# Products of constants on TensorE in the tails of the norms of a six-mixer network

## The chip, the cores and the metric

The kernel runs as one launch on one core of a Trainium2 chip. The metric is the device time of an execution in microseconds, lower is better. A core has a matrix engine (TensorE, here PE), a vector engine (VectorE, here DVE), a scalar engine (ScalarE, here ACT), a third elementwise engine (GpSimd, here POOL) and a queue for transfers (SyncE, here SP). Each engine works through its own instructions in the order in which they are written and stops only at waits for semaphores, which other engines count up.

## The reference

The reference passes 256 tokens of width 1024 through two layers of one block (a hybrid of a gated delta rule and attention, then a conformer convolution, each followed by a SwiGLU network) and four layers of a second (HGRN2, mLSTM, S5, HGRN2, each followed by a SwiGLU network). What matters here are the norms between these stages:

```python
def rms_norm(x, gain):
    xf = x.astype(F32)
    y = xf * lax.rsqrt(jnp.mean(jnp.square(xf), axis=-1, keepdims=True) + EPS)
    return (y * gain.astype(F32)).astype(x.dtype)
...
        h = h + gt1 * rms_norm(y, g_mix_post[layer])
        f = swiglu_ffn(modulate(rms_norm(h, g_ffn_pre[layer]), sh2, sc2), w_ffn_in[layer], w_ffn_out[layer])
        h = h + gt2 * rms_norm(f, g_ffn_post[layer])
...
def _layernorm(x, g, b):
    xf = x.astype(jnp.float32)
    mu = jnp.mean(xf, axis=-1, keepdims=True)
    xc = xf - mu
    var = jnp.mean(xc * xc, axis=-1, keepdims=True)
    return (xc * lax.rsqrt(var + LN_EPS) * g + b).astype(x.dtype)
```

In the first block a branch's output is normed and added to the residual, and the residual is normed again ahead of the next branch. In the second block the sum of residual and branch goes through one layer norm, and the result is the residual and the next input at once.

## The kernel before

Activations lie feature-major: eight chunks of 128 features on the partitions, 256 tokens along the free axis. A projection is a sum of products of a 128x128 weight tile with a 128x256 chunk. The weights come from memory in 341 slabs of 1 MB through a ring. Most projections split their operands in two fp32r parts: ACT rounds a slab (line 193), DVE forms the rest (line 219), and one product becomes three cheap matmuls (line 225). The remaining ones are plain fp32, and of these each product is two MATMUL records in the trace.

The program is a list of stages, and each engine gets each stage's instructions in that order. No planner is at work: what a stage's `tensor` function writes is what PE executes. PE has no other work beside the stage at hand, so when it waits in a norm, it is idle.

A norm's mean over features is a product with a constant matrix `mean` (all entries 1/1024), which leaves the mean on all partitions. There are these tails of stages:

- `OutProjection` (4 times, rms norm of a branch's output): the last two columns' products, then PE waits for ACT's square of the last chunk and adds the last product of the sum of squares (line 649). ACT forms the root (497, 503), DVE scales and adds to the residual (708, 712).
- `PreNorm` (3 times, directly behind an `OutProjection`): ACT squares the residual chunk by chunk (534), PE adds eight products with `mean` as the chunks come (552), then ACT forms the root, DVE scales (560), ACT and DVE form the two parts (544, 574), and the next stage's first products take them chunk by chunk. Ahead of `conformer` only the scaled input is formed, and the next products are plain fp32.
- `NormedProjection` (8 times, layer norm): behind the last column's products PE waits for DVE's last chunk of the sum (965) for the last product of the mean (854), then for its square for the last product of the mean of squares (856). DVE and ACT form variance and root (980, 897, 898), DVE centres and scales (984, 989), ACT and DVE form the parts (913, 997), in pairs of chunks. The next stage's first products wait for these. The eighth is the end of the network.
- `ConformerNorm` (once, inside the conformer): eight products for the mean as the convolution's chunks come (2574), DVE subtracts, ACT squares (2619), eight products for the variance (both line 2612), and then root, scale, SiLU and parts (2650).

The stages that follow a tail are `GateUp` (first projection of a SwiGLU network: its first slab is used for two outputs at once, so that each chunk that comes is used by six matmuls), `HgrnIn` and `MlstmIn` (the first slab is gone through twice, with three matmuls a chunk the first time), `S5In` and `ConformerIn` (plain fp32).

Of the kernel before, what the change touches and what calls it, by code (L numbers as in the profile page):

```python
# [23 lines left out]
KC = D // P  # L24
T = 256
# [317 lines left out]
        return flat.rearrange("p (a b c) -> p a b c", b=shape[1], c=shape[2])  # L343


def over_chunks(ap, n):

    return ap.unsqueeze(1).broadcast_to([ap.shape[0], n, ap.shape[1]])


def begin(eng, job):
    if job.before:
        eng.wait_ge(*job.before)


class Stage:
# [7 lines left out]
    def tensor(self, pe):  # L364
        pass

    def scalar(self, act):
        pass

    def vector(self, dve):  # L370
        pass
# [134 lines left out]
class PreNorm(Stage):  # L506
# [40 lines left out]

    def tensor(self, pe):
        begin(pe, self.job)
        for c in range(KC):  # L550
            pe.wait_ge(*self.squared[c])
            mm = pe.matmul(self.job.ap[:, 0:T], self.k.c("mean"), self.sq[:, c, :],  # L552
                           start=(c == 0), stop=(c == KC - 1))
        mm.then_inc(self.job.full[0], 1)

    def vector(self, dve):
        k = self.k
# [21 lines left out]
class OutProjection(Stage):  # L579
# [58 lines left out]
    def tensor(self, pe):  # L638
        chunkwise = 0
        if self.chunks == KC:  # L640
            first_columns(self, pe, self.out_jobs[0:2], self.order)
            chunkwise = 2
        for g, job in list(zip(self.groups, self.out_jobs))[chunkwise:]:
            begin(pe, job)
            for i, c in enumerate(g):
                mm = self.columns(pe, job.ap[:, i * T:(i + 1) * T], c)
            mm.then_inc(job.full[0], 1)
        pe.wait_ge(*self.y_squared[-1])
        pe.matmul(self.sum_job.ap[:, 0:T], self.k.c("mean"), self.sq[:, KC - 1, :], start=False, stop=True)\
          .then_inc(self.sum_job.full[0], 1)  # L650
# [82 lines left out]
def first_columns(stage, pe, jobs, order):  # L733

    k = stage.k
    for job in jobs:
        begin(pe, job)
    slab = [s.rearrange("p (k c) -> p k c", k=KC) for s in k.weights.next(pe)]
    for at, c in enumerate(order):
        pe.wait_ge(*stage.x_ready[c])  # L740
        for i, job in enumerate(jobs):
            mm = k.weights.product(pe, job.ap[:, 0:T], [s[:, c, i * P:(i + 1) * P] for s in slab],
                                   [x[:, c, :] for x in stage.x], at == 0, at == KC - 1)
            if at == KC - 1:
                mm.then_inc(job.full[0], 1)


class NormedProjection(Stage):
# [85 lines left out]
    def tensor(self, pe):  # L834
        k = self.k
        chunkwise = self.first_groups(pe)
        for g, job in list(zip(self.groups, self.out_jobs))[chunkwise:]:
            begin(pe, job)
            for i, c in enumerate(g):
                pause = self.early_sums if c == KC - 1 else None  # L840
                if self.glu:
                    self.columns(pe, job.ap[:, 0:T], 2 * c)
                    mm = self.columns(pe, job.ap[:, T:2 * T], 2 * c + 1, pause)
                else:
                    mm = self.columns(pe, job.ap[:, i * T:(i + 1) * T], c, pause)
                if c == g[-1]:
                    mm.then_inc(job.full[0], 1)
                if c == LATE:

                    begin(pe, self.shift_job)  # L850
                    pe.wait_ge(*self.shift_sum)
                    pe.matmul(self.shift_job.ap[:, 0:T], k.c("mean"), self.sq[:, 0, :], start=True, stop=True)                      .then_inc(self.shift_job.full[0], 1)
        pe.wait_ge(*self.y_late[-1])
        pe.matmul(self.mean_job.ap[:, 0:T], k.c("mean"), self.y[:, KC - 1, :], start=False, stop=True)          .then_inc(self.mean_job.full[0], 1)
        pe.wait_ge(*self.squared[-1])
        pe.matmul(self.var_job.ap[:, 0:T], k.c("mean"), self.sq[:, KC - 1, :], start=False, stop=True)          .then_inc(self.var_job.full[0], 1)

    def ahead(self, g):

        return -1 if g[0] < LATE else 0 if g[0] < KC - 2 else 1  # L860
# [59 lines left out]
    def vector(self, dve):  # L920
# [6 lines left out]
        for g, job, last in zip(self.groups, self.out_jobs, self.last_slab):  # L927
# [6 lines left out]
            if g[0] == LATE:  # L934

                dve.wait_ge(*self.shifted)
                dve.tensor_tensor(y[:, 0:4, :], y[:, 0:4, :], over_chunks(self.shift, 4), add)\
                   .then_inc(self.moved[0], 1)
                for c in range(LATE, KC):
                    ins = dve.scalar_tensor_tensor(y[:, c, :], k.h[:, c, :], ALPHA, self.shift, mult, add)  # L940
                chain.link(ins)
# [41 lines left out]
        def centre(first):  # L983
            return dve.tensor_tensor(y[:, first:first + 2, :], y[:, first:first + 2, :],  # L984
                                     over_chunks(self.mean_job.ap[:, 0:T], 2), subtract)
# [1598 lines left out]
class ConformerNorm(Stage):  # L2584
# [22 lines left out]
    def tensor(self, pe):  # L2607
        for job, src, ready in ((self.mean_job, self.x, self.x_ready), (self.var_job, self.sq, self.squared)):
            begin(pe, job)
            for c in range(KC):  # L2610
                pe.wait_ge(*ready[c])
                mm = pe.matmul(job.ap[:, 0:T], self.k.c("mean"), src[:, c, :], start=(c == 0), stop=(c == KC - 1))
            mm.then_inc(job.full[0], 1)

    def scalar(self, act):
        k = self.k
# [1484 lines left out]
```

## Time and profile before

| | |
|---|---|
| three runs | 2541.86, 2546.39 and 2548.13 us; median 2546.39 |
| span of the profiled execution | 2540.7 us |
| PE, PE weight load, DVE, ACT busy | 93%, 84%, 63%, 44% of the span |
| matmul records | 17410 |
| HBM traffic | 144 GB/s over the span |

The profile is of one execution of its own; of that one only the span is given. The span is 5.7 us below the median of the runs, which also holds the start and end of an execution. Busy PE time includes the modelled filling and emptying of the array. PEclk is the clock granted to TensorE: it takes two levels, 1.00 (2.4 GHz) and 0.50 (1.2 GHz), and a number in between is a mean over a stretch that holds both.

### The profile page before, as it was taken

The numbers are of one execution on the slowest core, as the hardware profiler recorded it, in microseconds if no ns is written. First come the engines' busy times: TensorE is split into PE (matmuls) and PEld (weight loads), VectorE is DVE, ScalarE is ACT, GpSimd is POOL, SyncE is SP. The second block draws the span as 40 slices with busy tenths as digits, with TensorE's granted clock in tenths as the row PEclk, the third lists the DMA queues.
The fourth block names the chain that finished last, engine by engine and source line by source line (L and its number), as shares of the span: only waits on it lengthen the run. The fifth ranks groups of instructions, "written<-read, shape, count | busy, mean of one in ns | idle before, by whom it ended". The sixth has DMA issues, their size and how long they took to land.

```text
span 2540.7 us, 41119 instructions
## 1 busy us (share of the span) xinstructions
PE 2355.5 (93%) x17410; PEld 2145.2 (84%) x17410; DVE 1597.9 (63%) x2601; ACT 1116.0 (44%) x1751; POOL 127.5 (5%) x130
## 2 busy tenths in 40 slices
PE   6998997999978999998998989998998998988997
PEld 3665687998868998998998869997678998987997
DVE  3376456654966545776656576556977656677655
ACT  2423235434254445634435445334555434835433
POOL 0012000000000000000000000003630000000000
PEclk9998998999989999978999889999999999978999
DMA  7246533553223554403553314542024554502551
GB/s 310 95 155 230 200 126 134 190 183 133 100 100 135 188 190 151 166 34 138 188 189 133 133 60 156 184 182 100 1 95 147 189 185 145 187 34 87 196 183 67
DMA packets 50296, 368.33 MB, mean 145 GB/s; under 512 B 5568, under 2 KB 5696, under 8 KB 5824
## 3 DMA queue, kind: packets, MB, share of 16 engines
q1 hardware_dynamic: 49968, 363.59, 39.2%
q8 instruction: 138, 2.26, 0.4%
q10 hardware_dynamic: 144, 2.10, 0.2%
q14 instruction: 46, 0.38, 0.0%
HBM read 364.62 MB, written 1.05 MB: 144 GB/s over the span
## 4 chain that ended last, share of the span: by engine, by line
PE 78%; DVE 14%; ACT 4%; issue 2%; DMA 1%; SPq 0%; DVEq 0%; ACTq 0%
PE psum L225 63%; DVE weight_parts L219 3%; PE psum L3007 2%; PE psum L3678 1%; PE psum L3679 1%; DMA weight_ring<-stream_dram 1%; PE psum L2524 1%; DVE work L989 1%; ACT weight_parts L193 1%; DVE work L984 1%; PE psum L552 1%; PE psum L407 1%; PE psum L3379 1%; PE psum L1629 1%; PE psum L3696 1%
## 5 line engine op out<-in xcount | busy, mean ns | idle before, releaser
L225 PE MATMUL psum<-input_parts,weight_parts 128*128 128x256 f32 x8448 | 1030.0, 285 | 47.4 <-DVE input_parts L997 27.0
L225 PEld LDWEIGHTS psum<-input_parts,weight_parts 128*128 128x128 f32 x8448 | 1023.5, 192 | 55.9 <-issue 50.2
L219 DVE TENSOR_TENSOR weight_parts<-weight_ring,weight_parts 128x1024 fp32r<-128x1024 f32 x536 | 631.9, 1220 | 272.7 <-ACT weight_parts L193 271.7
L193 ACT ACTIVATE weight_parts<-weight_ring 128x1024 fp32r<-128x1024 f32 x540 | 541.3, 1051 | 265.5 <-PE psum L225 265.0
L225 PE MATMUL psum<-hidden_parts,weight_parts 128*128 128x256 f32 x3936 | 479.5, 283 | 11.2 <-DVE hidden_parts L2650 6.6
L225 PEld LDWEIGHTS psum<-hidden_parts,weight_parts 128*128 128x128 f32 x3936 | 472.0, 190 | 16.3 <-issue 8.8
L1071 ACT ACTIVATE work<-psum 128x256 f32<-128x256 f32 x132 | 50.6, 384 | 422.9 <-PE psum L225 422.9
L1078 DVE TENSOR_TENSOR work<-work,psum 128x256 f32<-128x256 f32 x132 | 55.6, 421 | 282.8 <-ACT work L1071 282.8
L225 PE MATMUL psum<-work,weight_ring 128*128 128x256 f32 (+1 forms) x608 | 174.2, 445 | 3.5 <-ACT work L544 2.2
L225 PEld LDWEIGHTS psum<-work,weight_ring 128*128 128x128 f32 x608 | 117.2, 195 | 56.3 <-issue 43.2
L3007 PE MATMUL psum<-work 128*128 128x64 f32 x448 | 79.1, 364 | 3.6 <-DVE work L2845 3.6
L3007 PEld LDWEIGHTS psum<-work 128*128 128x128 f32 x448 | 78.5, 279 | 4.1 <-DVE work L2845 4.1
L225 PE MATMUL psum<-weight_parts,input_parts 128*128 128x256 f32 x576 | 70.3, 282 | 3.2 <-DVE weight_parts L219 3.2
L225 PE MATMUL psum<-weight_ring,silu_cond 128*32 128x256 f32 x768 | 56.3, 414 | 18.2 <-DMA weight_ring<-stream_dram 18.2
L225 PEld LDWEIGHTS psum<-weight_parts,input_parts 128*128 128x128 f32 x576 | 69.5, 188 | 3.8 <-issue 3.7
L2567 DVE SCALAR_TENSOR_TENSOR work<-work,vectors 128x256 f32<-128x256 f32 x168 | 67.2, 479 | 0.0
L3746 POOL TENSOR_TENSOR work<-constants,columns 128x256 f32<-128x256 f32 x32 | 19.6, 613 | 791.6 <-DVE work L3609 765.3
L1082 DVE TENSOR_TENSOR hidden_parts<-work,hidden_parts 128x256 fp32r<-128x256 f32 x132 | 56.2, 426 | 4.5
L3067 POOL MEMSET work<- 128x4096 f32 x2 | 7.0, 3514 | 985.1 <-DVE input_parts L723 720.6
L2824 ACT ACTIVATE work<-work 128x2048 f32<-128x2048 f32 (+1 forms) x16 | 29.1, 1819 | 51.3 <-DVE work L2833 45.9
L3678 PE MATMUL psum<-work,constants 128*128 128x256 f32 x128 | 39.7, 392 | 12.4 <-DVE work L3762 12.4
L865 ACT ACTIVATE work<-work 128x256 f32<-128x256 f32 (+2 forms) x32 | 20.2, 633 | 66.8 <-DVE work L965 52.1
(465 smaller groups left out, 2379.6 us busy)
## 6 DMA issues: line engine op xcount, KB each, us to landing
weight_ring<-stream_dram SPq DMA_DIRECT2D x341, 1024.0 KB, 4.8
constants<-constants_dram SPq DMA_DIRECT2D x1, 2176.0 KB, 14.5
work<-s_bc_dram ACTq DMA_DIRECT2D x1, 2048.0 KB, 8.9
work<-ctx_dram SPq DMA_DIRECT2D x1, 1024.0 KB, 6.9
residual<-x_dram SPq DMA_DIRECT2D x1, 1024.0 KB, 9.0
out_dram<-residual SPq DMA_DIRECT2D x1, 1024.0 KB, 3.9
vectors<-vectors_dram SPq DMA_DIRECT2D x1, 550.5 KB, 3.8
constants<-constants_dram SPq DMA_DIRECT2D x1, 65.0 KB, 3.5
```

The lines of the kernel that those rows point to most:

```text
L193: act.activation(self.parts[:, s % SPLITS, 0, cols], self.ring[:, i % RING, cols], ACT.Identity)\
L219: ins = dve.tensor_tensor(self.parts[:, s % SPLITS, 1, cols], self.ring[:, i % RING, cols], self.parts[:, s % SPLITS, 0, cols].bitcast(F32 ...
L225: mm = pe.matmul(*args, **kw)
L407: return pe.matmul(mod_columns(k, layer, n, 1), rows, k.c("strip_sum"), start=True, stop=True)
L552: mm = pe.matmul(self.job.ap[:, 0:T], self.k.c("mean"), self.sq[:, c, :], start=(c == 0), stop=(c == KC - 1))
L1071: act.activation(self.hid[:, j % 2, :], job.ap[:, 0:T], ACT.Silu).then_inc(self.silu[j][0], 1)
L1078: dve.tensor_tensor(hid, hid, (job if j else self.up_job).ap[:, T:2 * T], ALU.mult).then_inc(self.whole[j][0], 1)
L1082: dve.tensor_tensor(lo, hid, hi.bitcast(F32), ALU.subtract).then_inc(self.ready[j][0], 1)
L2567: ins = dve.scalar_tensor_tensor(acc, src, w, acc, ALU.mult, ALU.add)
L2824: act.activation(e, e, ACT.Exp).then_inc(self.exp[l][0], 1)
L3007: mm = pe.matmul(job.ap[:, at:at + P // 2], (e if b > 1 else kk)[:, h, cols], right, start=True, stop=True)
L3678: pe.matmul(out, k.c("ident"), t1[:, part, :], start=True, stop=False)
```

## The change

A function `idle_products(k, pe, n)` is added. It writes n products of two constants, `ident` (the stationary operand, 128x128) and the first 256 columns of `lower_pairs`, into the first 256 columns of PSUM bank `mod_bank`. Both operands are plain fp32. Nothing reads the result: the bank is used for the modulation vectors early in the program, and each place where the function is called in `PreNorm` and `OutProjection` stands behind a wait for the event `background.ready`, which DVE gives when it is done with that bank. The calls are, in each tail:

| stage | products of constants | in all |
|---|---|---|
| `OutProjection` x4 | 7 ahead of the last sum product | 28 |
| `PreNorm` x3 | 10 ahead of the first sum product, 1 ahead of each of the seven others, 10 behind the last | 81 |
| `NormedProjection` x8 | 9 ahead of the mean's last product; 12 behind the variance's last product, except at the end of the network | 156 |
| `ConformerNorm` x1 | 15 ahead of the mean's last product; 12 ahead of the first variance product and 1 ahead of each of the seven others; 20 behind the last | 54 |

That is 319 products. No other engine's instructions change.

```diff
--- before.py
+++ after.py
@@ -343,6 +343,12 @@
         return flat.rearrange("p (a b c) -> p a b c", b=shape[1], c=shape[2])
 
 
+def idle_products(k, pe, n):
+
+    for _ in range(n):
+        pe.matmul(k.mod_bank[:, 0:T], k.c("ident"), k.c("lower_pairs", 0, T), start=True, stop=True)
+
+
 def over_chunks(ap, n):
 
     return ap.unsqueeze(1).broadcast_to([ap.shape[0], n, ap.shape[1]])
@@ -547,11 +553,14 @@
 
     def tensor(self, pe):
         begin(pe, self.job)
+        pe.wait_ge(*self.k.background.ready)
         for c in range(KC):
+            idle_products(self.k, pe, 10 if c == 0 else 1)
             pe.wait_ge(*self.squared[c])
             mm = pe.matmul(self.job.ap[:, 0:T], self.k.c("mean"), self.sq[:, c, :],
                            start=(c == 0), stop=(c == KC - 1))
         mm.then_inc(self.job.full[0], 1)
+        idle_products(self.k, pe, 10)
 
     def vector(self, dve):
         k = self.k
@@ -645,6 +654,8 @@
             for i, c in enumerate(g):
                 mm = self.columns(pe, job.ap[:, i * T:(i + 1) * T], c)
             mm.then_inc(job.full[0], 1)
+        pe.wait_ge(*self.k.background.ready)
+        idle_products(self.k, pe, 7)
         pe.wait_ge(*self.y_squared[-1])
         pe.matmul(self.sum_job.ap[:, 0:T], self.k.c("mean"), self.sq[:, KC - 1, :], start=False, stop=True)\
           .then_inc(self.sum_job.full[0], 1)
@@ -850,10 +861,13 @@
                     begin(pe, self.shift_job)
                     pe.wait_ge(*self.shift_sum)
                     pe.matmul(self.shift_job.ap[:, 0:T], k.c("mean"), self.sq[:, 0, :], start=True, stop=True)                      .then_inc(self.shift_job.full[0], 1)
+        idle_products(k, pe, 9)
         pe.wait_ge(*self.y_late[-1])
         pe.matmul(self.mean_job.ap[:, 0:T], k.c("mean"), self.y[:, KC - 1, :], start=False, stop=True)          .then_inc(self.mean_job.full[0], 1)
         pe.wait_ge(*self.squared[-1])
         pe.matmul(self.var_job.ap[:, 0:T], k.c("mean"), self.sq[:, KC - 1, :], start=False, stop=True)          .then_inc(self.var_job.full[0], 1)
+        if self.next_slab < k.weights.count:
+            idle_products(k, pe, 12)
 
     def ahead(self, g):
 
@@ -2608,9 +2622,14 @@
         for job, src, ready in ((self.mean_job, self.x, self.x_ready), (self.var_job, self.sq, self.squared)):
             begin(pe, job)
             for c in range(KC):
+                if job is self.mean_job and c == KC - 1:
+                    idle_products(self.k, pe, 15)
+                if job is self.var_job:
+                    idle_products(self.k, pe, 12 if c == 0 else 1)
                 pe.wait_ge(*ready[c])
                 mm = pe.matmul(job.ap[:, 0:T], self.k.c("mean"), src[:, c, :], start=(c == 0), stop=(c == KC - 1))
             mm.then_inc(job.full[0], 1)
+        idle_products(self.k, pe, 20)
 
     def scalar(self, act):
         k = self.k
```

On PE, the tail of the first branch: `OutProjection` of the hybrid stage, its sum product (line 649 before, 660 now), `PreNorm`'s eight (552 before, 560 now), and the first gate and up products. Before:

```order
L225 MATMUL psum<-input_parts,weight_parts 128x256 x9
L649 MATMUL psum<-work,constants 128x256
L552 MATMUL psum<-work,constants 128x256 x8
L225 MATMUL psum<-input_parts,weight_parts 128x256 x1056
L225 MATMUL psum<-hidden_parts,weight_parts 128x256 x504
```

The same place now; line 349 is the product of constants:

```order
L225 MATMUL psum<-input_parts,weight_parts 128x256 x9
L349 MATMUL psum<-constants 128x256 x7
L660 MATMUL psum<-work,constants 128x256
L349 MATMUL psum<-constants 128x256 x10
L560 MATMUL psum<-work,constants 128x256
L349 MATMUL psum<-constants 128x256
L560 MATMUL psum<-work,constants 128x256
...
L349 MATMUL psum<-constants 128x256
L560 MATMUL psum<-work,constants 128x256
L349 MATMUL psum<-constants 128x256 x10
L225 MATMUL psum<-input_parts,weight_parts 128x256 x1056
```

Seven products of constants now stand between the last column and the sum product, seventeen ahead of and among the eight, and ten between the last of them and the first gate product.

On PE, the layer norm between the first SwiGLU network of the second block and mLSTM (lines 829 to 856 before, 843 to 868 now: the early and the last products of mean and variance). Before:

```order
L829 MATMUL psum<-work,constants 128x256
L832 MATMUL psum<-work,constants 128x256
L225 MATMUL psum<-hidden_parts,weight_parts 128x256 x24
L854 MATMUL psum<-work,constants 128x256
L856 MATMUL psum<-work,constants 128x256
L225 MATMUL psum<-input_parts,weight_parts 128x256 x48
```

The same place now:

```order
L843 MATMUL psum<-work,constants 128x256
L225 MATMUL psum<-hidden_parts,weight_parts 128x256 x24
L349 MATMUL psum<-constants 128x256 x9
L866 MATMUL psum<-work,constants 128x256
L868 MATMUL psum<-work,constants 128x256
L349 MATMUL psum<-constants 128x256 x12
L225 MATMUL psum<-input_parts,weight_parts 128x256 x48
```

Nine stand ahead of the mean's last product, twelve behind the variance's; the two products themselves stay together.

## Rows read from the trace of the kernel before

**Rows 1.** The page: span, busy time by engine, the chain's shares by engine.
```profile
span 2540.7 us, 41119 instructions
...
PE 2355.5 (93%) x17410; PEld 2145.2 (84%) x17410; DVE 1597.9 (63%) x2601; ACT 1116.0 (44%) x1751; POOL 127.5 (5%) x130
...
PE 78%; DVE 14%; ACT 4%; issue 2%; DMA 1%; SPq 0%; DVEq 0%; ACTq 0%
```

**Rows 2.** Groups by line and form, PE: count, busy us, mean ns, idle before.
```profile
L552 PE MATMUL psum<-work,constants 128*128 128x256 f32 x48 | 16.8, 526 | 8.4 <-ACT work L534 8.4
...
L854 PE MATMUL psum<-work,constants 128*128 128x256 f32 x16 | 6.6, 502 | 5.0 <-DVE work L965 5.0
...
L649 PE MATMUL psum<-work,constants 128*128 128x256 f32 x8 | 3.3, 502 | 2.0 <-ACT work L658 2.0
```

**Rows 3.** Chain in order of time, end of the network ahead of mLSTM.
```profile
1352.89 0.43 PE psum L829 x2
```

**Rows 4.** PE's timeline, ConformerNorm: start us, length us, what, idle before.
```profile
712.95 3.19 PE L2612 MATMUL psum<-work,constants 128*128 128x256 f32 x14
720.13 1.22 PE L2612 MATMUL psum<-work,constants 128*128 128x256 f32 x2 [3.99 <-DVE work L2574]
724.73 5.59 PE L2612 MATMUL psum<-work,constants 128*128 128x256 f32 x16 [3.38 <-ACT work L2619]
736.92 24.11 PE L225 MATMUL psum<-hidden_parts,weight_parts 128*128 128x256 f32 x183 [6.60 <-DVE hidden_parts L2650]
```

**Rows 5.** PE's timeline, layer norm ahead of mLSTM.
```profile
1357.12 0.70 PE L854 MATMUL psum<-work,constants 128*128 128x256 f32 x2 [0.51 <-DVE work L965]
1357.66 0.61 PE L856 MATMUL psum<-work,constants 128*128 128x256 f32 x2
1362.36 1.62 PE L225 MATMUL psum<-input_parts,weight_parts 128*128 128x256 f32 x6 [4.09 <-DVE input_parts L997]
1364.58 1.65 PE L225 MATMUL psum<-input_parts,weight_parts 128*128 128x256 f32 x6 [0.59 <-DVE input_parts L997]
1366.88 6.05 PE L225 MATMUL psum<-input_parts,weight_parts 128*128 128x256 f32 x36 [0.66 <-DVE input_parts L997]
```

**Rows 6.** PE's timeline, layer norms behind mLSTM, ahead of S5 and behind S5.
```profile
1530.12 7.68 PE L225 MATMUL psum<-input_parts,weight_parts 128*128 128x256 f32 x48 [4.09 <-DVE input_parts L997]
1538.33 11.89 PE L225 MATMUL psum<-input_parts,weight_parts 128*128 128x256 f32 x96 [0.52 <-DVE weight_parts L219]
...
1726.40 13.84 PE L225 MATMUL psum<-residual,weight_ring 128*128 128x256 f32 x50 [3.03 <-ACT residual L903]
...
1930.67 0.70 PE L854 MATMUL psum<-work,constants 128*128 128x256 f32 x2 [1.39 <-DVE work L965]
1931.47 0.70 PE L856 MATMUL psum<-work,constants 128*128 128x256 f32 x2
```

**Rows 7.** PE's timeline, OutProjection and PreNorm of the first two pairs.
```profile
416.25 1.22 PE L649 MATMUL psum<-work,constants 128*128 128x256 f32 x2 [0.47 <-ACT work L658]
420.28 5.92 PE L552 MATMUL psum<-work,constants 128*128 128x256 f32 x16 [2.80 <-ACT work L534]
429.08 16.19 PE L225 MATMUL psum<-input_parts,weight_parts 128*128 128x256 f32 x113 [2.88 <-DVE input_parts L574]
...
629.98 14.05 PE L225 MATMUL psum<-work,weight_ring 128*128 128x256 f32 x64 [2.23 <-ACT work L544]
```

**Rows 8.** Stretches behind ten norms at low clock: length, busy per engine, PEclk, DMA.
```profile
429.00:435.00 6.00, 5.92 (x28) 5.95 (x29) 5.57 (x13) 4.57 (x9) 0.00 (x0) 0.50 0.01 3
736.90:742.20 5.30, 5.28 (x25) 5.30 (x26) 2.89 (x7) 5.30 (x13) 0.00 (x0) 0.50 0.66 247
...
1726.40:1732.10 5.70, 5.70 (x14) 4.53 (x15) 4.12 (x12) 3.58 (x10) 0.00 (x0) 0.50 0.19 40
...
2135.20:2145.10 9.90, 8.55 (x36) 8.00 (x37) 9.08 (x25) 6.05 (x14) 3.52 (x1) 0.50 0.07 11
...
sum 61.60, PE 57.79 PEld 55.10 DVE 55.74 ACT 36.43 POOL 5.44; mean PE 5.78 PEld 5.51 DVE 5.57 ACT 3.64 POOL 0.54
```

## The prediction

> **What bounds the kernel now.** I read the page first. PE is busy for 93% of the span and carries 78% of the chain that ended last, DVE 14% [rows 1]. So the norms are the places where the chain leaves PE and comes back. Then the groups of PE's instructions by line, for the idle time ahead of each sum product: 5.0 us in all ahead of L854 in the eight layer norms, 2.0 us ahead of L649 in the four output projections, 8.4 us ahead of L552 in the three PreNorms [rows 2]. Third, PE's timeline in each tail. The two kinds of wait differ widely: about 0.5 us between the last column and the sum product [rows 5, 7], but 2.8 us ahead of PreNorm's sums, 4.09 us between the variance and the next projection, 6.60 us at the end of ConformerNorm [rows 4, 5, 7]. Last, the table of stretches: behind ten norms PE works at a granted clock of 0.50 (1.2 GHz), for 57.79 us of busy time in all [rows 8]. The engine had idled some 3 to 7 us just before each. That low clock is all that products of constants could remove.
>
> **The price of one product of constants.** The trace of before has no product with both operands constant, but it has the same instruction form: fp32, 128x128 stationary, 256 columns, two records. At full clock one takes 0.43 us on the chain [rows 3], and seven in a row with the same stationary matrix take 3.19 us, which is 7 x 0.43 plus 0.18 for emptying the array [rows 4]. At low clock 14 records take 5.70 us, 0.81 us a product [rows 8]. I take 0.43: the trace shows no discount for a repeated stationary operand. A product follows its predecessor without the 0.18 us, so n of them ahead of a wait of w delay what stands behind it by 0.43n - 0.18 - w.
>
> **Part 1: ahead of the sums.** What is added here delays the norm itself, and everything follows from the norm.
> - Layer norm, 9 products: 3.87 - 0.18 - 0.5 = 3.2 us. L856 stood 0.54 us behind L854 [rows 5] and can now follow at 0.43, which gives 0.1 back: 3.1 us in each of seven. Behind S5 the wait is 1.39 us and the second gap 0.80 [rows 6]: 3.69 - 1.39 - 0.37 = 1.9. Together 7 x 3.1 + 1.9 = 23.6 us.
> - Output projection, 7 products: 3.01 - 0.18 - 0.5 = 2.3 us, four times: 9.3 us.
> - PreNorm, 10 products against 2.80 us: 4.30 - 0.18 - 2.80 = 1.3 us. Then eight sums with seven products between: 15 x 0.43 + 0.18 = 6.6 us against 16.8 / 3 = 5.6 now [rows 2], so 1.0 us more. Three times 2.3: 7.0 us.
> - ConformerNorm: 15 products against 3.99 us: 6.45 - 0.18 - 3.99 = 2.3 us, less 0.5 since the product behind it takes 0.70 at full clock instead of 1.22 [rows 4, 5]: 1.8. Then 12 against 3.38: 1.6. Then 6.6 instead of 5.59: 1.0. Together 4.4 us.
>
> Sum of part 1: 23.6 + 9.3 + 7.0 + 4.4 = 44.3 us.
>
> **Part 2: behind the sums, and the clock.** 12 products start the next projection 5.16 - 0.18 - 4.09 = 0.9 us late, ahead of S5 (wait 3.03) 1.95 us, 10 behind PreNorm 1.25 us (conformer, wait 2.23: 1.9), 20 in ConformerNorm 1.8 us. Against it stands a clock that stays high: an fp32r matmul takes 0.215 us at low clock (28 in 5.92, 25 in 5.28, [rows 8]) and 0.12 at full (96 in 11.89, [rows 6]). Which ends last must be asked for each follower.
> - GateUp behind a layer norm (4): the first slab's 48 matmuls took 7.68 us half at low clock, and then PE still waited 0.52 us for DVE's weight parts, 8.2 us behind the start [rows 6]. These come by the norm's time, not by PE's. Neither the 0.9 us nor the clock counts: 0.
> - mLSTM and the second HGRN2: chunks come in pairs, the last 36 matmuls start 4.5 us behind the first and took 6.05 us [rows 5]; at full clock 36 x 0.12 = 4.3, so 1.7 us back. In the second HGRN2 the low clock lasts 9.9 us [rows 8], 5.3 us past the start of the last 36: 25 x 0.215 + 11 x 0.12 = 6.6 us, of which 2.3 come back. Together -4.0. The 0.9 us is gone by the second pair.
> - S5, fp32, PE-bound: 5.70 us at 0.81 instead of 0.43 give 2.7 back, 1.95 lost: -0.75.
> - First gate product behind the first PreNorm: 28 x 0.215 + 20 x 0.12 = 8.3 us before [rows 7, 8]; now 1.25 + 48 x 0.12 = 7.0: -1.3. Behind ConformerNorm 25 at low clock and 23 at full, 8.1; now 1.8 + 5.8 = 7.6: -0.5. The two other PreNorms have no low stretch behind them: +1.9 and +1.25.
> - The first HGRN2 has no products of constants behind the sum; its low clock stays: 0.
>
> Sum of part 2: -4.0 - 0.75 - 1.3 - 0.5 + 3.15 = -3.4 us.
>
> **Total.** 44.3 - 3.4 = 40.9 us on the profiled execution's 2540.7 us span [rows 1], which is 2581.6. The median of the runs lies 5.7 us above that span; I leave this as it is: 2546.4 + 40.9 = 2587.3 us, 1.6% slower.
>
> Bounds. Part 1 varies with the clock at which the nine or seven products run: in some tails the sums stand at low clock already. L649 at 416.25 took 1.22 us, L854 in the tail ahead of mLSTM 0.70 [rows 5, 7], and 6.6 us for eight of L854 [rows 2] is six of 0.70 and two of 1.22. These tails could cost 1 us more each or, once the clock is up, 0.9 us less. Some 247 of the 319 products are felt, so that 0.02 us in the price is 5 us. Part 2 could be as low as -12 (all low stretches gone, below) and as high as +5 (the clock falls again in the 2 us waits between pairs, nothing is returned in mLSTM, HGRN2 and S5). That is +30 to +56 us on 2546.4; with a few us for the measurement 2574 to 2606.
>
> **Two rules of the Trainium skill.** Between the layer norm's last column and L854 the row shows PE idle for 0.51 us [rows 5], with nothing else that could run. The page "TensorE: Matmul & The Clock Gate", section "Step-by-step: what each phase is for", says that weight loads may be pulled ahead but matmuls stay in program order. By that rule the mean's product can't overtake nine idle ones even when its operand is ready, and the sum stays at 44.3; were they overtaken it would be about zero. The same page, section "Why this matters for your kernels", asks to avoid long PE gaps between bursts because the clock goes back to half. The rows agree that low stretches follow the idle of the tails [rows 4, 5, 8]. By that rule alone all of them vanish; that is rival C.
>
> **The rivals.**
> - A, not slower: the products are cheap. If two constants with a repeated stationary operand went through at the fp32r price of 0.12 us, then nine cost 1.08 - 0.18 - 0.5 = 0.4 us, seven 0.2 us, the loops of sums would end with ACT's last square, 1.3 us earlier in each of four, and the rest would hide in the waits. 8 x 0.3 + 4 x 0.2 - 4 x 1.3 - 0.5 = -2.5 us, and some of the 2.7 us in S5: 2542 us. It decides below 0.43 - 40.9 / 247 = 0.26 us a product. Against it: seven with the same stationary matrix take 3.19 us [rows 4]. 5%.
> - B, far slower: products of mostly zeros don't count as work for the clock. Then it falls in the tails as before, and the products behind the fall cost twice. All 319 at 0.43 us more are 137 us, 178 with the 40.9; the first seven or so of some twelve tails still run at full clock, 36 us less, so between 142 and 178: near 2706 us. For it: no product of two constants is in the trace, so it can't be excluded. Against it: the fp32 sums in PreNorm and S5's fp32 products keep or bring the clock up like the others (PE's stretch at 0.50 ahead of S5 ends after 5.70 us of them, [rows 8]), and these have the same shape. 8%.
> - C, all the low clock is returned: 57.79 us of busy time would shrink by 1 - 0.12 / 0.215 = 0.44, 25.5 us, with part 2's delays all felt (5.4 + 1.95 + 2.5 + 1.9 + 1.8 = 13.6): 44.3 + 13.6 - 25.5 = 32.4, 2579 us. Against it: the wait for weight parts behind the first slab [rows 6]. 12%.
> - D, part of the delay is taken up by waits downstream that don't hang on the norm (weights that now come in time): up to 9 us, also near 2578 us. Against it: the wait that I found for weight parts is for DVE, which is itself in the norm. 8%.
>
> My forecast has 67%. Measured differences of under 0.3% (7.6 us) can't be told from no change here. Forecast, B, C and D are all slower: 95%, of which I leave 1% to errors of the whole account. A lies within 0.3% more often than below it: same 4%, faster 2%. The range 2572 to 2608 holds forecast, C and D, and leaves out A and B, 13%, and a few per cent of the rest.
>
> **What would show it.** The trace should have 638 more matmul records, 18048. A line for them near 0.43 us each at full clock, L349. The mean's last product (now L866) should start 3.7 us behind the last column with no idle time ahead of it, in eight places; the sum product L660 2.8 us behind its column, in four. PE should wait 0.5 us or less between the variance and the next projection. Clock 1.00 in nearly all stretches behind norms, except in the first HGRN2. DVE's wait for weight parts at 8.2 us behind the start of GateUp should stay. I am wrong if L349 runs below 0.26 us, if PEclk in the tails is still 0.50, or if the distance from last column to the variance's end grows by less than 2 us per layer norm.

## The result and the profile after

The change makes the kernel slower, about as forecast.

| | before | changed |
|---|---|---|
| runs, median | 2547.26 us (4 runs, 2541.86 to 2552.41) | 2586.43 us (4 runs, 2582.06 to 2591.89) |
| ratio | | 1.0169, 95% interval 1.0148 to 1.0191 |
| span of the profiled execution | 2540.7 us | 2587.2 us |
| matmul records | 17410 | 18048 |

The forecast was 2587.3 us. The range of 2574 to 2606 us holds all four runs. First the page of the changed kernel, to be read against [rows 1]: span, busy time, granted clock in 40 slices, the chain.

```profile
span 2587.2 us, 42394 instructions
...
PE 2460.4 (95%) x18048; PEld 2247.5 (87%) x18048; DVE 1597.8 (62%) x2601; ACT 1115.8 (43%) x1751; POOL 127.5 (5%) x130
...
PEclk9998999999999999979999889999999999969999
...
PE 79%; DVE 13%; ACT 4%; issue 2%; DMA 1%; SPq 0%; DVEq 0%; ACTq 0%
```

The clock line of the kernel before, which [rows 1] leaves out:

```profile
PEclk9998998999989999978999889999999999978999
```

The mean granted clock rose from 0.946 to 0.965. DVE, ACT and POOL did the same work in the same time. PE is busy 105 us more (what the products add, less what the better clock takes off), and the span is 46.5 us longer. So some 58 of the 105 us fell into time in which PE had waited, and the rest did not. The groups of PE's instructions give the price:

```profile
L349 PE MATMUL psum<-constants 128*128 128x256 f32 x638 | 147.2, 379 | 0.0
...
L866 PE MATMUL psum<-work,constants 128*128 128x256 f32 x16 | 4.7, 378 | 0.0
```

L866 is the layer norm's last mean product (L854 before, [rows 2]): 5.0 us of idle time ahead of it have become 0.0. It isn't PE that waits for its operand any more, its operand waits for PE. The timeline of the tail ahead of mLSTM, against [rows 5]:

```profile
1386.73 4.05 PE L349 MATMUL psum<-constants 128*128 128x256 f32 x18
1390.61 0.59 PE L866 MATMUL psum<-work,constants 128*128 128x256 f32 x2
1391.04 0.59 PE L868 MATMUL psum<-work,constants 128*128 128x256 f32 x2
1391.48 5.34 PE L349 MATMUL psum<-constants 128*128 128x256 f32 x24
1396.47 1.06 PE L225 MATMUL psum<-input_parts,weight_parts 128*128 128x256 f32 x6
1397.96 1.02 PE L225 MATMUL psum<-input_parts,weight_parts 128*128 128x256 f32 x6 [0.43 <-DVE input_parts L1011]
1400.27 4.63 PE L225 MATMUL psum<-input_parts,weight_parts 128*128 128x256 f32 x36 [1.28 <-DVE input_parts L1011]
```

Nine products start at 1386.73 and the mean's product at 1390.61: 3.88 us for nine, 0.43 each. Behind the sums the next projection starts 5.43 us after the start of the variance's product, with no wait; before it took 4.70 us with one [rows 5], so PE is now some 0.7 us late there. The clock is up: six matmuls take 1.06 instead of 1.62 us, the last 36 take 4.63 instead of 6.05. But PE then waits 1.28 instead of 0.66 us for the last chunks, which is where part of what the clock gives goes. Two signs that the prediction named are met: the mean's product 3.7 us behind the last column's end, and no wait between the variance and the next projection.

The tail of the first branch, against [rows 7]:

```profile
419.62 3.22 PE L349 MATMUL psum<-constants 128*128 128x256 f32 x14
422.69 0.59 PE L660 MATMUL psum<-work,constants 128*128 128x256 f32 x2
423.12 4.48 PE L349 MATMUL psum<-constants 128*128 128x256 f32 x20
427.44 0.59 PE L560 MATMUL psum<-work,constants 128*128 128x256 f32 x2
427.87 0.59 PE L349 MATMUL psum<-constants 128*128 128x256 f32 x2
...
433.91 4.48 PE L349 MATMUL psum<-constants 128*128 128x256 f32 x20
438.04 2.23 PE L225 MATMUL psum<-input_parts,weight_parts 128*128 128x256 f32 x16
```

From 419.62 to the first gate product at 438.04 there is no idle time at all. PE sets the pace of a stretch in which it used to wait for ACT and DVE.

A layer norm with GateUp behind it (after mLSTM), against [rows 6]:

```profile
1560.27 0.59 PE L866 MATMUL psum<-work,constants 128*128 128x256 f32 x2
...
1566.12 3.23 PE L225 MATMUL psum<-input_parts,weight_parts 128*128 128x256 f32 x24
1569.92 3.09 PE L225 MATMUL psum<-input_parts,weight_parts 128*128 128x256 f32 x24 [0.57 <-DVE input_parts L1011]
1573.60 6.62 PE L225 MATMUL psum<-input_parts,weight_parts 128*128 128x256 f32 x51 [0.59 <-DVE weight_parts L219]
```

PE works faster and waits more: 0.57 us for chunks, and again over half a microsecond for DVE's weight parts. The second slab's matmuls start 7.5 us behind the first's, where the prediction had 8.2, because PE starts later; from the mean's last product they stand 13.3 us, against 13.4 before (from 1524.89 to 1538.33). They come by the norm's time.

The clock in the place of one of the stretches of [rows 8], shifted with the program, in the table of stretches:

```profile
1396.40:1404.40 8.00, 6.29 (x48) 5.82 (x48) 7.33 (x15) 5.86 (x13) 0.00 (x0) 1.00 0.01 3
```

It is 1.00 there, with 48 matmuls in it instead of 28. Of ten such stretches nine are at 1.00; the one behind the output projection ahead of the first HGRN2, the only tail with no products behind its sum, is not.

To compare kernels I cut each tail in three by the starts of PE's matmuls: from the last one ahead of the sum product to the sum product (wait 1), from there to the next projection's first (norm), and over the next 100 matmuls (entry). In `ConformerNorm` the first of the mean's eight products counts as the sum product, so that its waits are all in the norm part. The records of two kernels correspond one to one when the products of constants are left out. Sums over thirteen tails, us:

| kernel, profile | wait 1 | norm | entry | together | against before |
|---|---|---|---|---|---|
| before | 10.9 | 103.9 | 199.2 | 314.0 | |
| before, second profile | 10.8 | 100.7 | 200.6 | 312.2 | -1.8 |
| changed | 45.4 | 123.6 | 184.6 | 353.6 | +39.6 |
| changed, second profile | 47.4 | 123.6 | 185.8 | 356.7 | +42.8 |

The span less these tails lies between 2223 and 2237 us in the twelve profiles of this document, with the changed kernel's two at 2233.6 and 2223.2 and the two of before at 2227 and 2229. A difference of some us outside the tails says nothing.

### The profile page after: what moved, and what is told of

Its sections match the earlier page's. It is cut to its first block, busy times and chain, and to the rows that moved or that the text cites. A ratio compares the mean times of both kernels' runs of the same rounds, so it can differ in the third digit from the quotient of the medians.

```text
span 2587.2 us, 42394 instructions
## 1 busy us (share of the span) xinstructions
PE 2460.4 (95%) x18048; PEld 2247.5 (87%) x18048; DVE 1597.8 (62%) x2601; ACT 1115.8 (43%) x1751; POOL 127.5 (5%) x130
## 4 chain that ended last, share of the span: by engine, by line
PE 79%; DVE 13%; ACT 4%; issue 2%; DMA 1%; SPq 0%; DVEq 0%; ACTq 0%
PE psum L225 61%; PE psum L349 3%; DVE weight_parts L219 3%; PE psum L3026 2%; PE psum L3697 1%; PE psum L2538 1%; PE psum L3698 1%; DMA weight_ring<-stream_dram 1%; DVE work L1003 1%; ACT weight_parts L193 1%; PE psum L413 1%; DVE work L998 1%; PE psum L3398 1%; DVE input_parts L1011 1%; PE psum L1643 1%
## 5 line engine op out<-in xcount | busy, mean ns | idle before, releaser
L225 PE MATMUL psum<-input_parts,weight_parts 128*128 128x256 f32 x8448 | 1018.8, 283 | 21.3 <-DVE weight_parts L219 9.7
L225 PEld LDWEIGHTS psum<-input_parts,weight_parts 128*128 128x128 f32 x8448 | 1011.1, 190 | 27.6 <-issue 17.8
L349 PE MATMUL psum<-constants 128*128 128x256 f32 x638 | 147.2, 379 | 0.0
L349 PEld LDWEIGHTS psum<-constants 128*128 128x128 f32 x638 | 120.1, 190 | 16.7
## 6 DMA issues: line engine op xcount, KB each, us to landing
constants<-constants_dram SPq DMA_DIRECT2D x1, 2176.0 KB, 14.4
```

The source lines that it names most:

```text
L225: mm = pe.matmul(*args, **kw)
L349: pe.matmul(k.mod_bank[:, 0:T], k.c("ident"), k.c("lower_pairs", 0, T), start=True, stop=True)
```

## The experiments

Theory S is the prediction's: a product costs 0.43 us of PE's time in program order, n of them ahead of a wait w delay all behind by 0.43n - 0.18 - w, and only a clock that stays high stands against it. N is the rival that the time comes from the products' traffic wherever they stand, K that it is lost behind the sums. All ratios are to the kernel before, with their 95% interval; the us behind a ratio are worked out from it.

**e1_ahead**: only the products ahead of the short waits.

```diff
-            idle_products(self.k, pe, 10 if c == 0 else 1)      # PreNorm
-        idle_products(self.k, pe, 10)
-        if self.next_slab < k.weights.count:                    # NormedProjection
-            idle_products(k, pe, 12)
-                    idle_products(self.k, pe, 15)               # ConformerNorm
-                    idle_products(self.k, pe, 12 if c == 0 else 1)
-        idle_products(self.k, pe, 20)
```

> Keeps only the 9 products ahead of the mean's last product in the eight layer norms and the 7 ahead of the sum product in the four output projections (100 products), all of which stand ahead of a wait of about 0.5 us (1.4 us behind S5). Theory S (a product costs 0.43 us of PE's time in program order, so n of them ahead of a wait w delay all behind by 0.43n - 0.18 - w, and against it stands only the clock that stays high): 7 x 3.1 + 1.9 + 4 x 2.3 = 32.8 us, less 2 to 3 us for low stretches that become shorter: +28 to +33 us against before. Rival N (the time comes from the products' traffic, wherever they stand: 39 us over 319 products, 0.12 us each): +12 us. Rival K (the loss comes from the places behind the sums, where PE is late for the next projection): about 0.

Measured: ratio 1.0130 (1.0110 to 1.0150), +33 us. Tails: wait 1 47.2, norm 101.4, entry 199.5, together +34.2, at the upper end of what S allows. All of it is in wait 1. The timeline ahead of mLSTM shows no wait left ahead of the mean's product, and behind the sums the wait of [rows 5] to 0.01 us:

```profile
1369.15 4.05 PE L349 MATMUL psum<-constants 128*128 128x256 f32 x18
1373.03 0.59 PE L864 MATMUL psum<-work,constants 128*128 128x256 f32 x2
...
1378.16 1.62 PE L225 MATMUL psum<-input_parts,weight_parts 128*128 128x256 f32 x6 [4.10 <-DVE input_parts L1007]
```

100 of the 319 products carry most of the loss; N's +12 and K's 0 fall.

**e2_behind**: only the products behind the last sum of each norm (12, 10, 20).

```diff
-        idle_products(self.k, pe, 7)                            # OutProjection
-        idle_products(k, pe, 9)                                 # NormedProjection
-            idle_products(self.k, pe, 10 if c == 0 else 1)      # PreNorm
-                    idle_products(self.k, pe, 15)               # ConformerNorm
-                    idle_products(self.k, pe, 12 if c == 0 else 1)
```

> Keeps only the products behind the last sum of each norm: 12 in seven layer norms, 10 in three PreNorms, 20 in ConformerNorm (134 products). Theory S: they are 0.9 to 1.95 us too long for their waits, but this is either hidden behind DVE's weight parts or more than paid by the clock: -3 to -8 us against before. Rival N: 134 x 0.12 = +16 us. Rival K: most of the +39 us is here. If the clock is low in these stretches all the same, +8 to +13 us.

Measured: ratio 1.0001 (0.9982 to 1.0019). Tails: +1.5 us (norm +14.7, entry -13.7). More products than in e1_ahead, and no loss: N and K fall again. But I had expected a gain. In the four layer norms ahead of GateUp the tails took 21.85, 20.80, 22.01 and 21.03 us against 21.84, 20.80, 22.02 and 21.85: neither late products nor the better clock is felt, as the prediction had it. Where the clock was low at the start the products cost more, as PE's timeline shows behind the first HGRN2. Twelve products take 6.51 us from the first's start to the next matmul, instead of the 4.99 us of the tail ahead of mLSTM; the rest of that tail gave this back:

```profile
1172.24 6.86 PE L349 MATMUL psum<-constants 128*128 128x256 f32 x24
1178.75 11.43 PE L225 MATMUL psum<-input_parts,weight_parts 128*128 128x256 f32 x92
```

**e8_middle**: the rest, 85 products ahead of and among PreNorm's and ConformerNorm's sums.

```diff
-        idle_products(self.k, pe, 7)                            # OutProjection
-        idle_products(self.k, pe, 10)                           # PreNorm, behind
-        idle_products(k, pe, 9)                                 # NormedProjection
-        if self.next_slab < k.weights.count:
-            idle_products(k, pe, 12)
-        idle_products(self.k, pe, 20)                           # ConformerNorm, behind
```

> Keeps only the products that neither e1_ahead nor e2_behind has: 10 ahead of PreNorm's first sum and 1 ahead of each of the seven others, 15 ahead of the mean's last product in ConformerNorm, 12 ahead of its first variance product and 1 ahead of each of the others (85 products in four tails). Theory S: 3 x (1.3 + 1.0) + 4.3 = 11 us in those four tails, less 1 to 2 us for sums at full clock: +8 to +11 us, so that the three parts (+34, +1.5 and this) add up to the change's +40 to +45 us. Rival K2 (the parts are not additive, a late PE ahead of the sums hides what stands behind them): 5 us or less. Rival N (0.12 us for each product wherever it stands): +10 us as well; this run doesn't tell N apart, e1_ahead and e2_behind do.

Measured: ratio 1.0069 (1.0047 to 1.0092), +17.6 us; tails +12.1 (norm +12.7), the four tails alone +12.5. That is above the +8 to +11 that I expected, by 1 us in the tails and by more in the runs, whose interval is +12 to +23 us. K2's 5 us or less falls. The three parts' tails are 34.2 + 1.5 + 12.1 = 47.8 us, the whole change's 39.6 and 42.8: together they cost 5 to 8 us less than one by one. The likely reason is that only together do they keep the clock up through all of a tail; no run isolates it, and the tails of one kernel differ by 2 to 3 us from profile to profile. The ratios of the parts say 1.0130, 1.0001, 1.0069, which add up to +51 us, with intervals of 5 to 6 us to either side of each.

**e9_eighteen**: e1_ahead with 18 instead of 9 ahead of the mean's last product.

```diff
-        idle_products(k, pe, 9)
+        idle_products(k, pe, 18)
```

> As e1_ahead, with 18 instead of 9 products ahead of the mean's last product in the eight layer norms. Theory S: nothing covers the second nine, so that each costs its whole 0.43 us: 8 x 9 x 0.43 = +31 us on top of e1_ahead's +33, +64 us against before, the mean's last product 7.88 us behind the last column instead of 4.0. Rival (the engine's queue lets part of them pass beside the wait or DVE's and ACT's work absorbs some): less than +50 us.

```profile
1378.63 7.93 PE L349 MATMUL psum<-constants 128*128 128x256 f32 x36
1386.40 0.59 PE L864 MATMUL psum<-work,constants 128*128 128x256 f32 x2
```

Measured: ratio 1.0263 (1.0230 to 1.0297), +67 us; tails +64.4, where +64 was expected. The timeline ahead of mLSTM shows 18 products in 7.77 us and the mean's product right behind them, 7.89 us behind the last column's start where 7.88 was expected: linear, with nothing passing.

**e3_half**: all 319 products over 128 columns. **e5_two**: over 2 columns.

```diff
-        pe.matmul(k.mod_bank[:, 0:T], k.c("ident"), k.c("lower_pairs", 0, T), start=True, stop=True)
+        pe.matmul(k.mod_bank[:, 0:P], k.c("ident"), k.c("lower_pairs", 0, P), start=True, stop=True)   # e3_half
+        pe.matmul(k.mod_bank[:, 0:2], k.c("ident"), k.c("lower_pairs", 0, 2), start=True, stop=True)   # e5_two
```

> All 319 products, each over 128 columns instead of 256. Theory S: 0.21 us each, so that nine of them are 1.9 us against 0.7 us that the wait covers: +1.2 us in each of seven layer norms, +0.8 in each of four output projections, PreNorm's loop ends earlier than before, the clock stays high as in the changed kernel: -2 to +5 us against before. The lateness per product is linear in the columns. Rival N, if the number counts: +39 us; if the columns count: +20 us.

> All 319 products, each over 2 columns. Two records then take about 0.22 us, since the weight loads set the pace (L407 in the kernel before: 0.11 us a record), the same as the 128-column products of e3_half, but the array hardly works. Theory S: the lateness ahead of the sums is that of e3_half (+14 us in the thirteen tails), and the clock falls in the tails as before, so what e3_half got back (7.4 us from the sum product to 100 matmuls behind the next start) is lost: +13 to +17 us in the tails, 7 us more than e3_half. Rival C (the clock is worth 20 us or more, and e3_half hid this behind other losses): +25 us or more. If 2 columns keep the clock up as well as 128: the same as e3_half.

Measured: e3_half 1.0051 (1.0032 to 1.0070), +13 us; tails +7.0 (wait 1 +14.4, norm -4.7, entry -2.7). e5_two 1.0148 (1.0120 to 1.0176), +38 us; tails +43.8 (wait 1 +15.5, norm +25.8, entry +2.4). e3_half missed: my range was -2 to +5 us. Wait 1 grew by 14.4 us where the expectation had 11.6, in part because two layer norms were reached at low clock, and what comes back behind it is 7.4 us, the low end of the 7 to 14 that the range took. The runs' interval, +8 to +18 us, lies above the tails' +7 as well; where the rest is stays open. It still excludes N's +20 and +39. e5_two is far off: I expected it 7 us above e3_half, it is 37. Wait 1 shows that a 2-column product costs about the same as one of 128 while the clock is high. The groups of e3_half:

```profile
L349 PE MATMUL psum<-constants 128*128 128x128 f32 x638 | 81.4, 278 | 0.0
```

and of e5_two, with PreNorm's sums (L560) and a stretch through ConformerNorm from the table of stretches:

```profile
L349 PE MATMUL psum<-constants 128*128 128x2 f32 x638 | 109.0, 298 | 0.0
...
L560 PE MATMUL psum<-work,constants 128*128 128x256 f32 x48 | 28.5, 698 | 0.6 <-ACT work L540 0.6
...
735.00:763.00 28.00, 27.91 (x115) 26.36 (x116) 10.77 (x15) 16.71 (x33) 0.00 (x0) 0.51 0.07 26
...
750.67 8.53 PE L349 MATMUL psum<-constants 128*128 128x2 f32 x40
```

PE is busy for 27.91 of 28 us, at a granted clock of 0.51. In the kernel before the clock was 0.73 over `ConformerNorm` (713 to 745 us), with PE busy for 18 of 32 us; in e3_half it was 1.00. So the clock is worse here than without any products, which I had not expected, and everything in the stretch costs double: 20 products take 8.53 us, as long as 20 of 256 columns take at full clock, and PreNorm's sums 28.5 us in all instead of 16.8 [rows 2]. 33 of the 37 us are in ConformerNorm and the three PreNorms with the output projections ahead of them, where products stand among the sums. That is what the clock is worth when PE has been made the bound. With its waits left alone it is worth much less.

**e4_fit** and **e6_some**: only products that fit into their waits.

```diff
-        idle_products(self.k, pe, 7)                                     # OutProjection
+        if self.split:                                                   # e6_some alone, behind the sum
+            idle_products(self.k, pe, 9)
-        idle_products(k, pe, 9)                                          # NormedProjection
-            idle_products(k, pe, 12)
+            idle_products(k, pe, 9 if self.split else 7)                 # e6_some: not ahead of GateUp
-            idle_products(self.k, pe, 10 if c == 0 else 1)               # PreNorm
+            idle_products(self.k, pe, 6 if c == 0 else 0)
-        idle_products(self.k, pe, 10)
+        idle_products(self.k, pe, 6 if self.split else 5)
-                    idle_products(self.k, pe, 15)                        # ConformerNorm
+                    idle_products(self.k, pe, 9)
-                    idle_products(self.k, pe, 12 if c == 0 else 1)
+                    idle_products(self.k, pe, 7 if c == 0 else 0)
-        idle_products(self.k, pe, 20)
+        idle_products(self.k, pe, 15)
```

> Only products that fit into their waits by 0.43n - 0.18 < w: none ahead of the waits of 0.5 us and none inside the loops of sums; 9 behind the variance (7 ahead of S5), 6 ahead of PreNorm's first sum and 6 behind its last (5 in front of the conformer's projection), 9, 7 and 15 in ConformerNorm: 127 products. Theory S: nothing is delayed and the clock stays high: -9 to -13 us against before (S5 -2.7, first gate products -1.5 to -3, ConformerNorm -3 to -4, mLSTM and HGRN2 -1 to -4). Rival N: +15 us. If products of constants take the clock's benefit away or bring none, 0.

> As e4_fit, but without the nine products in the layer norms ahead of GateUp, where DVE's weight parts set the next slab's time, and with nine behind the output projection ahead of the first HGRN2 (wait 4.49 us). Theory S: the gains of e4_fit stay (first tail -1.8, ConformerNorm -0.9, S5 -1.6, second HGRN2 -0.8), the loss behind mLSTM (+1.0, nine products caught at low clock) goes: -4 to -7 us in the tails, a ratio of 0.997 to 0.9985. Rival (fillers bring nothing at all once other waits are counted): 1.000.

Measured: e4_fit 0.9998 (0.9983 to 1.0013), tails -3.4 us; e6_some 0.9994 (0.9978 to 1.0010), tails -4.0. The loss is gone with the products that didn't fit, as S says. The gain is a third of what I expected of e4_fit, at the edge of what I expected of e6_some, and too small to be told from none: a second profile of the kernel before differs by 1.8 us. Two places in e4_fit say where it went. In ConformerNorm, PE and ACT:

```profile
726.00 3.72 PE L2628 MATMUL psum<-work,constants 128*128 128x256 f32 x16 [0.27 <-ACT work L2636]
728.00 1.99 ACT L193 ACTIVATE weight_parts<-weight_ring 128x1024 fp32r<-128x1024 f32 x2
...
730.00 1.28 ACT L503 ACT_TABLE_LOAD   x1
731.30 0.47 ACT L503 ACTIVATE work<-psum,epsilons 128x256 f32<-128x256 f32 x1
```

The sums took 3.72 us instead of 5.59 and ended at 729.7. But ACT rounds weights until 730.0 and then loads a table, so that the root starts at 731.30. In the kernel before the sums ended at 730.32, the table load at 729.92 and the root started at 730.36: there were 0.4 us to gain, not the 1.9 that the sums became shorter. And behind mLSTM, PE:

```profile
1522.55 0.67 PE L839 MATMUL psum<-work,constants 128*128 128x256 f32 x2 [2.93 <-DVE work L987]
...
1527.68 5.57 PE L349 MATMUL psum<-constants 128*128 128x256 f32 x18
1532.90 3.20 PE L225 MATMUL psum<-input_parts,weight_parts 128*128 128x256 f32 x24
```

Nine products that would take 3.87 us at full clock took 5.2: the granted clock was 0.50 from 1524 to past 1530 us, and the norm part of that tail grew from 5.24 to 7.09 us. A count that fits at full clock doesn't fit at low clock. The clock had fallen ahead of the products, behind an idle time of 2.93 us ahead of L839 and one of 0.51 us ahead of the mean's product, and they fill neither.

**e0_before** and **e7_after**: both kernels once more, unchanged.

> The kernel before, unchanged, for a second profile. The thirteen tails, each from the last matmul ahead of the sum product to 100 matmuls behind the next start, sum to 314.0 us in the first profile. Theory S: within 3 us of that, since the waits are fixed and only the clock's falls move; the rest of the program may differ by several us, as the 7 us of the change's profile outside its tails do.

> The changed kernel, unchanged, for a second profile. Its tails summed to 353.6 us. Theory S: within 3 us of that, and the difference to a second profile of before again 38 to 41 us, whatever the spans' difference is.

Spans 2540.9 and 2579.9 us. Their tails, in the table above, are within 3.2 us of the first profiles', where I had expected 3; the difference of the second pair is 44.6 us, 3.6 above my range. Outside the tails the changed kernel was 6.9 us longer than before in the first pair and 5.6 us shorter in the second, so that part is scatter and not the change's.

## Why the prediction was right

Step by step, from the first profiles; the parts by the starts of the matmuls:

| step | predicted | measured | second profiles |
|---|---|---|---|
| price of one product at full clock | 0.43 | 3.88 / 9 = 0.43 | |
| layer norms, ahead of and between the last sums (8) | +23.6 | +22.9 | +24.5 |
| output projections (4) | +9.3 | +9.5 | +10.9 |
| PreNorm, ahead of and among the sums (3) | +7.0 | +6.3 | +6.9 |
| ConformerNorm up to its last sum | +4.4 | +4.4 | +5.2 |
| part 1 | +44.3 | +43.1 | +47.5 |
| part 2, all behind the sums | -3.4 | 39.6 - 43.1 = -3.5 | 44.6 - 47.5 = -2.9 |
| thirteen tails | +40.9 | +39.6 | +44.6 |

- Matmuls stay in order. That the mean's product can't pass the nine is what made the sum; e9_eighteen shows it with eighteen.
- The position decides, not the number alone: 100 products ahead of short waits cost 33 us in e1_ahead, 134 behind the sums cost nothing that shows in e2_behind.
- The clock stays up almost everywhere: rival B (2706 us) is out. Rival A (0.12 us a product) is out by the price. Rival C (all low stretches return their time, 2579 us) had the clock right and the worth wrong, as argued: GateUp's entry is set by DVE's weight parts. Rival D has nothing for it: outside the tails the changed kernel's two profiles average the same 2228 us as the two of before. Up to some 5 us of it would be lost in the scatter there.
- Part 2 held as a sum, and in that there is luck. Its terms, each from the start of the last sum product (the variance's, in layer norms) to 100 matmuls behind the next projection's start:

| behind the sums | predicted | first profiles | second profiles |
|---|---|---|---|
| GateUp behind a layer norm (4) | 0 | -0.9 | -0.1 |
| mLSTM | -1.7 | -1.4 | -2.1 |
| second HGRN2 | -2.3 | -2.2 | -0.2 |
| S5 | -0.75 | -0.9 | -0.6 |
| first PreNorm | -1.3 | -0.6 | 0.0 |
| second PreNorm (conformer) | +1.9 | +1.8 | +0.2 |
| third PreNorm | +1.25 | -0.1 | 0.0 |
| ConformerNorm | -0.5 | 0.0 | 0.0 |
| first HGRN2 | 0 | +0.8 | -0.1 |

  The third PreNorm's term was wrong: I took the late start as fully felt, and almost nothing of it was (norm +1.1 behind the sums, entry -1.15): the entry became shorter by as much as the start was late. Five of the nine terms are off by 0.5 to 1.3 us in the first profiles, and the errors cancel. Single terms move by up to 2 us between the two pairs, as the granted clock does from execution to execution: behind the second PreNorm of the kernel before it was 1.00 in the first profile (630 to 642 us) and 0.86 in the second (634 to 646). So the trace of one execution can't give part 2 term by term.
- What the prediction's part 2 doesn't show is how little there was to gain. My expectations for e2_behind, e3_half and e4_fit took several us too much for the same clock, for the reasons read above: chunks that come in pairs, DVE's weight parts, ACT's table load.

The median of the runs moved by 39.2 us, the ratio says +38 to +49, and 40.9 lies with both. The mechanism is shown; that the forecast median was met within 1 us is luck, since single runs of one kernel differ by 10 us and the two pairs of profiles by 5. Nor are the 5.7 us between span and median the start and end of an execution alone: where both are on record for one execution they differ by 1.8 to 1.9 us, so the profiled execution of before was also a short one.

## What to carry to other kernels

Products that only keep the clock up are work in program order: count them against the wait at the very place, here 0.5 us against nine times 0.43, and not against the idle time of the stage. Ahead of a statistic on which everything waits nothing is hidden. Before filling a gap ask what the low clock costs behind it: where the next matmuls are fed by another engine, a faster PE only waits more, and the counts must also fit at the low clock.

## What the runs showed of the hardware that was not expected

- In e5_two PE was busy for 27.91 of 28 us, 78 of its 115 matmul records over 2 columns, and the granted clock was 0.51. At the low clock a two-column product costs double as well: 20 take 8.53 us, 0.42 each from start to start, against 0.21 in the tails at full clock. That it is the weight load that sets this pace is likely, since 2 and 128 columns cost about the same, but no run isolates it.
- In the changed kernel products of two constants, mostly zeros, follow each other for 8.4 us behind ConformerNorm's sums, and the granted clock was 1.00 over the whole stretch from 736 to 766 us.
- The same fp32r matmuls at a granted clock of 1.00 come at one of three paces, fixed through a stage and different from stage to stage and run to run. For the six stages that are a SwiGLU network's matmuls, in twelve profiles, the mean start-to-start time without the waits was 117.3 to 117.5, 118.6 to 118.7 or 119.9 to 120.0 ns and nothing else. The first SwiGLU stage in the kernel before, and the same stage in the changed kernel, in the table of stretches:

```profile
460.00:600.00 140.00, 140.00 (x1196) 140.00 (x1195) 77.93 (x104) 57.52 (x76) 0.00 (x0) 1.00 0.52 188
```

```profile
470.00:610.00 140.00, 140.00 (x1169) 140.00 (x1168) 76.25 (x101) 55.35 (x74) 0.00 (x0) 1.00 0.50 181
```

  1196 and 1169 matmuls in the same 140 us. Over the some 12000 such matmuls of the kernel one step is 17 us, and this is probably most of the scatter between runs. What sets the pace stays open.
